# RWKV-7 chunk recurrence in 64x64 TensorE tiles, with the loop's own instructions ahead of the work placed beside it

## The chip, the cores and the metric

The program runs on one core of one Trainium2 chip. The metric is the device time of one execution in microseconds (us), as the median of the runs.

## What is computed

One encoder layer on 1024 tokens of width 1024: a projection, multi-head latent attention (8 heads) beside RWKV-7 time mixing (8 heads of 64), an output projection, cross-attention to 256 memory tokens, an MLP, and a final norm. The change touches the RWKV-7 recurrence alone:

```python
def wkv7(r, decay, k, v, a, b):
    def step(state, inp):
        rt, wt, kt, vt, at, bt = inp
        sa = jnp.einsum('bhvk,bhk->bhv', state, at)
        state = state * wt[:, :, None, :] + sa[..., None] * bt[:, :, None, :] + vt[..., None] * kt[:, :, None, :]
        return state, jnp.einsum('bhvk,bhk->bhv', state, rt)
```

The kernel doesn't step through 1024 tokens. It works in 16 chunks of 64 tokens: inside a chunk a triangular 64x64 system is solved, and from chunk to chunk the 64x64 state of each head is carried by a product with a matrix M and the addition of a matrix N.

## The kernel before, in words

All of it is written out by hand as one instruction stream for each engine. The engines meet through counted semaphores: `Steps` holds the order of named steps of one engine, `r_at(L_DVE, "st1_4")` waits for a step. Each engine works strictly in order, so a wait holds up all that stands behind it in that engine's list.

The eight heads are four *pairs* (p = 0 to 3), and a pair's two heads lie in the lower and upper 64 partitions. A pair has 8 *windows* of 128 tokens (two chunks), two windows make a *group*, so a pair has four groups g0 to g3 of four chunks each, and the loop has 16 groups. In a group TensorE (PE) does, in this order:

- `solve` (L1381): the block inverse of the two windows times their tokens; ACT copies the result (L2089).
- `local`, `other_r`, `carry` (L1392 to L1455): 56 products of 64x64 (two instructions each) that make R and Y (what the outputs read) and M and N (stacked in 128 rows, for the carry). ACT copies R and Y (L2094); DVE adds the diagonal of decays to M and N (`mt`, L2768). The diagonals (`dg`, L902) are made by POOL.
- four chunks k = 0 to 3: `state` and `outputs` (L1457, L1469) with tiles of 128x64, the old state copied by DVE into `rST` (L2778), between them the preparation of the next group: the two doubling steps of the block inverse (`double_q`, `double_z`, with masks and adds by DVE, L2741 and L2750), `scores` in k = 0 and 1 (masked by DVE, L2624), `tokens` in k = 2 and 3 (three 128x128 transposes and one product a window, copied by ACT, L1961 to L1964), and `a_v` after k = 3 (copied by ACT, L1969).

Beside this run the *slots*. Slots 0 to 43 of pair p's loop hold the preparation of pair p+1 (`prep(p + 1, s)`) and the finish of pair p-1 (`post(p - 1, s - 22)`); slots 0 to 3 of a pair are reached at the end of the group before it. For the last pair `memory_step` stands in them. Each engine calls `beside(p, s)` for each slot at its own place in its list. With t = 11 g the places are: t+4 before `local`; t+5 and t+6 before chunk 0 (DVE: t+4 and t+5 before `mt`, t+6 after it); then two slots in each chunk (`places`: t+7 + 2k and t+8 + 2k). The slots that the prediction speaks of:

- 0 to 3: PE `lw0`, `lw1`, `la0`, `la1` (L1228, one 512-column product each, into one PSUM bank, so that each waits until ACT has read the one before, L1902 and L1906); 3 DVE `kk`, `t1p`, `L`.
- 5 to 7: ACT `kksq` (L1912), PE `ks0`, `ks1` (L1231), ACT `kl0`, `kl1` (L1917). 10, 11: ACT `W`, `kf`, `Wi` (L1923, L1925, L1928), the first with a table load.
- 14 to 17: DVE `nkk`, `at`, `b`, `bt`, `kt` (L2532 to L2549). 18, 19: PE `al` (L1276) on what `bt` made, DVE masks it (L2559); then SP stores it to DRAM and reads it back in blocks.
- 26 to 30 (`SUBST`): 15 steps of two small DVE operations (L2582, L2585) and one copy (L2588): the inverse of the 16x16 blocks. SP carries it through DRAM into the tile that `double_q` of the next pair reads in g3.
- 28, 29, 32: `post` 6, 7, 10: PE L1231, ACT L1951 and L1955. 33, 34: PE `rk0`, `rk1` (L1231), DVE `bv` (L2594).
- 37 to 39: `post` 15 to 17: DVE `yn`, `yb` (L2608, L2611), PE `lg0`, `lg1` (L1228), DVE `out` (L2618).

Of the kernel before, what the change touches and what calls it, by code (L numbers as in the profile page):

```python
# [12 lines left out]
ALU = mybir.AluOpType  # L13
# [14 lines left out]
SUBST = {26: (0, 1, 2, 3), 27: (4, 5, 6, 7), 28: (8, 9, 10, 11), 29: (12, 13), 30: (14,)}  # L28
# [91 lines left out]
RP_SET = 6  # L120
# [48 lines left out]
def build(nc, x_t, mem_t, pos, wall, vecs, con_d, headw, wv_d, lora_d, out_t):  # L169
    with ExitStack() as ctx:  # L170
# [29 lines left out]
        rsm = sb("rsm", [HD, 64])  # L200
# [50 lines left out]
        rWT = [rsm[:, 32 * n:32 * n + 32].rearrange("p (c h) -> p c h", h=2) for n in range(2)]  # L251
# [10 lines left out]
        rAG, rBK, rVZ, rPG = ([wbuf(n, k).rearrange("p (h n) -> p h n", h=2) for n in range(2)] for k in range(4))  # L262
        rRY = [wbuf(n, 4).rearrange("p (c h n) -> p c h n", c=2, h=2) for n in range(2)]
# [3 lines left out]
        rDg, rMT = ssum[:, 0:512], ssum[:, 512:1024]  # L267
        rST = tmp[:, :, :].rearrange("p a (c h n) -> p (a c) h n", h=2, n=HD)
# [257 lines left out]
        P_ACT = Steps(sem("prep_act"), each(["tw0", "tw1", "ta0", "ta1", "kksq", "kl0", "kl1", "W", "kf", "Wi", "wt0", "wt1", "afirst"]))  # L526
# [7 lines left out]
        l_pe, l_act, l_dve, l_pool = ["sc0_0", "sc0_1", "tok0_0", "tok0_1", "akv0_0", "akv0_1"], [], ["sc0_0", "sc0_1"], []  # L534
        l_act += [f"{x}0_{w}" for w in range(2) for x in ("ag", "bk", "vz")] + [f"akv0_{w}" for w in range(2)]
# [4 lines left out]
        for p in range(PAIRS):  # L540
            for g in range(NW // 2):
                ab = [f"{p}_{2 * g + k}" for k in range(2)]
                more = g < NW // 2 - 1 or p < PAIRS - 1
                nx = [f"{p}_{2 * g + 2 + k}" if g < NW // 2 - 1 else f"{p + 1}_{k}" for k in range(2)]
                for x in ("pg", "ry"):
                    l_act += [f"{x}{v}" for v in ab]
                l_pe += [f"{x}{v}" for x in ("pg", "lo") for v in ab] + [f"{x}{v}" for v in ab for x in ("ry", "mn")]
                l_pool += [f"dg{v}" for v in ab]
                l_dve += [f"mt{p}_{g}"]
                for k in range(4):  # L550
                    c = 4 * g + k
                    if c < NC - 1:
                        l_dve += [f"st{p}_{c}"]
                    l_pe += ([f"y{p}_{c}", f"st{p}_{c}"] if k == 0 else
# [5 lines left out]
                    if more and k < 2:  # L560
                        l_dve += [f"sc{nx[k]}"]
                    if k == 3:
                        l_act += [f"y{p}_{g}"]
# [2633 lines left out]
```

## Time and profile before

| | us |
|---|---|
| median of 3 runs | 1725.84 (1721.74 to 1727.79) |
| the profiled execution's own time | 1721.01 |
| its span | 1718.9 |
| PE busy | 1651.7 (96%) |
| DVE busy | 1122.1 (65%) |
| ACT busy | 869.8 (51%) |
| POOL busy | 767.1 (45%) |
| the recurrence loop with what leads into it | 437 to 712.6 |

The page gives one execution: how long each engine had an instruction in work, the chain of work that ended last, and the groups of instructions that cost most. For a change inside the loop the shares over the span say little. What is read here is the timeline of single groups, where the stretch from one `solve` (L1388) to the next is the time of a group. A PE instruction's time holds about 0.2 us in which it is under way in the array, so the pitch of its instructions has to be taken from starts, or from a run of x instructions less the length of one. An fp32 product is two instructions.

### The profile page before, as it was taken

The page shows a single profiled execution, that of the slowest core. Times are in us where ns is not written, and L with a number is a line of the kernel's source. Part 1 is how long each engine was busy: PE and PEld are TensorE (multiplying, and loading weights), DVE is VectorE, ACT ScalarE, POOL GpSimd, SP SyncE. Part 2 cuts the span into 40 slices and gives each one's busy share as a digit, 9 for nine tenths or more (in the row PEclk, how much of TensorE's full clock was granted, in tenths as well). Part 3 has the DMA queues.
Part 4 walks back from the last instruction along what each step waited for, and adds up shares of the span by engine and source line. Part 5 has one row for each costly group of instructions (what it writes and reads, how often), then busy time and mean ns, then how long its engine had stood idle before and what let it go on. Part 6 is the DMA issues. An engine that isn't in the chain of part 4 may idle for free.

```text
span 1718.9 us, 30289 instructions
## 1 busy us (share of the span) xinstructions
PE 1651.7 (96%) x11840; PEld 1275.3 (74%) x11840; DVE 1122.1 (65%) x1728; ACT 869.8 (51%) x1687; POOL 767.1 (45%) x555
## 2 busy tenths in 40 slices
PE   8999999988989888999999999999999999999997
PEld 6676777655666567688977677788888888888886
DVE  8744344336466675633687769887858866784788
ACT  5323333354425444511453467766667566666763
POOL 4210212011211012313493257868768695867771
PEclk9999999998899999999999999999999999999999
DMA  6100010001121223332302003020202212120202
GB/s 242 37 25 22 25 47 1 22 6 37 27 56 28 47 40 112 136 111 73 111 25 74 1 1 98 14 86 26 74 27 72 63 37 92 31 74 25 74 1 98
DMA packets 82841, 94.45 MB, mean 55 GB/s; under 512 B 53776, under 2 KB 56336, under 8 KB 82704
## 3 DMA queue, kind: packets, MB, share of 16 engines
q1 hardware_dynamic: 82704, 92.57, 17.2%
q8 instruction: 93, 1.52, 0.4%
q14 instruction: 44, 0.36, 0.1%
HBM read 82.57 MB, written 9.98 MB: 54 GB/s over the span
## 4 chain that ended last, share of the span: by engine, by line
PE 77%; DVE 12%; ACT 4%; issue 3%; DMA 2%; POOL 2%; SPq 0%; DVEq 0%; ACTq 0%; POOLq 0%
PE PS L1727 39%; PE PS L1054 8%; PE PS L969 5%; PE PS L1155 3%; PE PS L1194 2%; PE PS L1173 2%; PE PS L1683 2%; PE PS L1228 2%; PE PS L1519 1%; PE PS L1661 1%; PE PS L1231 1%; POOL sa L917 1%; DVE H L2915 1%; PE PS L1363 1%; DVE xn L2333 1%
## 5 line engine op out<-in xcount | busy, mean ns | idle before, releaser
L1727 PE MATMUL PS<-memr,wsp 128*128 128x512 f32 x1488 | 357.6, 391 | 1.4 <-DVE memr L2897 1.4
L1727 PEld LDWEIGHTS PS<-memr,wsp 128*128 128x128 f32 x1488 | 278.7, 188 | 63.6 <-DVE memr L2897 3.6
L932 POOL TENSOR_TENSOR wsp<-sa,wsp 128x512 fp32r<-128x512 f32 x120 | 165.9, 1386 | 167.4 <-ACT wsp L2155 167.2
L1727 PE MATMUL PS<-memr,wraw_r 128*128 128x512 f32 x744 | 181.6, 393 | 0.5 <-DVE memr L2897 0.5
L1727 PEld LDWEIGHTS PS<-memr,wraw_r 128*128 128x128 f32 x744 | 140.5, 189 | 31.6 <-DVE memr L2897 1.2
L1727 PE MATMUL PS<-tmp_r,wsp 128*128 128x512 f32 x564 | 147.2, 395 | 2.5 <-DVE tmp_r L2897 2.3
L1054 PE MATMUL PS<-xn,wsp 128*128 128x512 f32 x576 | 146.3, 400 | 2.4 <-DVE proj L2378 1.5
L2897 DVE TENSOR_TENSOR memr<-PS,memr 128x512 fp32r<-128x512 f32 x185 | 126.2, 682 | 33.8 <-ACT PS L2193 33.8
L823 POOL CAST wsp<-wraw 128x1024 fp32r<-128x1024 f32 x24 | 28.2, 1175 | 239.2 <-PE PS L1054 112.5
L2915 DVE TENSOR_TENSOR H<-PS,H 128x512 f32<-128x512 f32 x160 | 108.2, 686 | 40.3 <-PE PS L1727 24.3
L1862 ACT ACTIVATE H<-PS,mst 128x128 f32<-128x128 f32 (+3 forms) x64 | 47.4, 741 | 165.1 <-DVE mst L2462 165.1
L1054 PEld LDWEIGHTS PS<-xn,wsp 128*128 128x128 f32 x576 | 104.4, 188 | 35.3 <-issue 15.7
L1727 PEld LDWEIGHTS PS<-tmp_r,wsp 128*128 128x128 f32 x564 | 105.4, 188 | 28.2 <-DVE tmp_r L2897 4.0
L2184 ACT CAST memr<-sa 128x512 fp32r<-128x512 f32 x114 | 70.3, 617 | 109.1 <-PE PS L1727 74.5
L932 POOL TENSOR_TENSOR wraw_r<-sa,wraw_r 128x512 fp32r<-128x512 f32 x64 | 88.4, 1384 | 52.8 <-ACT wraw_r L2155 52.8
L969 PE MATMUL PS<-xn,wsp 128*128 128x512 f32 x480 | 109.9, 390 | 1.1 <-issue 1.1
L917 POOL TENSOR_TENSOR sa<-sa 128x512 f32<-128x512 f32 x64 | 92.2, 1443 | 34.1 <-DMA sa<-in_weights_dram 32.2
L969 PEld LDWEIGHTS PS<-xn,wsp 128*128 128x128 f32 x480 | 90.0, 188 | 20.6 <-issue 2.0
L2193 ACT COPY PS<-sa 128x512 f32<-128x512 f32 x175 | 102.0, 583 | 3.1 <-DVE con_r L2897 1.8
L2462 DVE TENSOR_REDUCE mst<-PS 128x1 f32<-128x128 f32 (+3 forms) x64 | 48.2, 754 | 83.2 <-PE PS L1158 83.0
L2841 DVE TENSOR_TENSOR sa<-sa 128x512 f32<-128x512 f32 x80 | 93.9, 1176 | 6.6 <-ACT sa L2134 6.6
L932 POOL TENSOR_TENSOR wsp<-sbx,wsp 128x512 fp32r<-128x512 f32 x66 | 88.6, 1344 | 11.1 <-ACT wsp L2155 11.1
(384 smaller groups left out, 3438.1 us busy)
## 6 DMA issues: line engine op xcount, KB each, us to landing
sa<-in_weights_dram SPq DMA_DIRECT2D x40, 512.0 KB, 4.3
wraw<-in_weights_dram SPq DMA_DIRECT2D x24, 512.0 KB, 3.8
sa<-in_weights_dram SPq DMA_DIRECT2D x48, 256.0 KB, 2.8
H<-in_x_dram SPq DMA_DIRECT2D x16, 512.0 KB, 7.1
sbx<-in_weights_dram SPq DMA_DIRECT2D x32, 256.0 KB, 2.9
H<-in_weights_dram SPq DMA_DIRECT2D x8, 512.0 KB, 6.9
out_dram<-sbx SPq DMA_DIRECT2D x16, 256.0 KB, 2.1
a_dram<-H SPq DMA_DIRECT2D x16, 128.0 KB, 2.5
```

Source lines behind the costliest of these rows:

```text
L917: nc.gpsimd.tensor_tensor(out, a, b, op).then_inc(W_SUM.sem, W_SUM.one(name))
L932: nc.gpsimd.tensor_tensor(w[:, 1, :], w_source(g), w[:, 0, :].bitcast(F32), ALU.subtract).then_inc(mw_rest, 1)
L969: last = nc.tensor.matmul(PS[:, bank + half, :], wsp[:, k, kt, a, :], src[:, at, b, HALF * half:HALF * half + HALF], start=(i == 0 and (a, ...
L1054: last = nc.tensor.matmul(PS[:, bank, :], wsp[:, u % 2, kt, a, :], xn[:, kt, b, HALF * half:HALF * half + HALF], start=(kt == 0 and (a, b) ...
L1155: nc.tensor.matmul(PS[:, b + part, 0:n], mQ[:, win(q)], mK[:, HALF * part:HALF * part + n], start=True, stop=(part < q // 4))
L1727: last = nc.tensor.matmul(PS[:, bank_of(g), :], w[:, a, win(k)], x[:, b, :], start=(k == 0 and (a, b) == (0, 0)), stop=(k == ROWS - 1 and ...
L2184: nc.scalar.copy(x_split_of(d)[:, 0, :], x_source(d)).then_inc(mx_head, 1)
L2193: nc.scalar.copy(PS[:, PS_BANKS + d % 2, :], x_source(d)).then_inc(mx_staged, 1)
L2462: m(nc.vector.tensor_reduce(mNeg[h % 2][:, q:q + 1], two(2 * (q % 2))[:, 0:P * (q + 1)], AX_X, ALU.max, negate=True), f"m{h}_{q}")
L2841: nc.vector.tensor_tensor(out, a, b, op).then_inc(X_SUM.sem, X_SUM.one(name))
L2897: nc.vector.tensor_tensor(x[:, 1, :], source, x[:, 0, :].bitcast(F32), ALU.subtract).then_inc(mx_rest, 1)
L2915: out(nc.vector.tensor_tensor(tile, a, b, ALU.add), f"{kind}{part}_{v}")
```

## The change

- Every product of the recurrence becomes 64x64. A head's state lies in its own 64 partitions; `state` multiplies it by M alone and adds to N, which `given(p, c)` has summed into the same bank just before (4 products a chunk). The decay is no longer a diagonal in M: DVE multiplies the old state by it while it adds the bank (`scalar_tensor_tensor`). POOL's `dg` is gone, and M is copied by ACT (`mt`).
- `local`, `other_r` and `carry` become `carry(p, g)` (M and the local outputs, 24 products) and `reads(p, g)` (8 products), which go round the four tiles. R gets its r by an addition on DVE (`r`), Y by one on DVE at k = 3 (`y`) instead of ACT's copy.
- `scores`, `tokens` and `a_v` take a whole group at once, in k = 0, 1 and 2. `tokens` is 32 products with the identity or the mean filter instead of 6 transposes and 2 products. ACT copies with four instructions of 256 columns and one for `a_v`, and does it ahead of the slots of that chunk; DVE masks the scores with one instruction of 768 columns at k = 0, ahead of the slots.
- `places`: t+5 and t+6 come with t+7 and t+8 behind chunk 0. t+4 stays ahead of it, on DVE behind `r`. The substitution moves from slots 26 to 30 to slots 27 to 30.

```diff
-SUBST = {26: (0, 1, 2, 3), 27: (4, 5, 6, 7), 28: (8, 9, 10, 11), 29: (12, 13), 30: (14,)}
+SUBST = {27: (0, 1, 2, 3), 28: (4, 5, 6, 7), 29: (8, 9, 10, 11), 30: (12, 13, 14)}
...
-            return range(11 * g + 7 + 2 * k, 11 * g + 9 + 2 * k)
+            return range(11 * g + (7 + 2 * k if k else 5), 11 * g + 9 + 2 * k)
...
+            def quad(out, h, c, left, right, start, stop):
+                return nc.tensor.matmul(PS[HD * h:HD * h + HD, out[0], out[1]:out[1] + CH], left, right, start=start, stop=stop)
...
+            def carry(p, g):
+                for s in range(2):
+                    r_at(L_ACT, f"pg{p}_{2 * g + s}")
+                    for h, c in QUADS:
+                        quad((c, CH * s), h, c, rPG[s][chunk(c), h, 0:HD], rBKs[g % 2][chunk(c), s, 0, cols(h)], True, True)
+                    for h, c in QUADS:
+                        quad((c, P + CH * s), h, c, rPG[s][chunk(c), h, HD:P], rSC[s][chunk(c), h, 0, :], True, False)
+                    for h, c in QUADS:
+                        last = quad((c, P + CH * s), h, c, rVs[g % 2][chunk(c), s, h, :], rSC[s][chunk(c), h, 2, :], False, True)
+                last.then_inc(L_PE.sem, L_PE.one(f"mn{p}_{g}"))
...
+            def given(p, c):
+                n, s = c % 2, c // 2 % 2
+                if c % 4:
+                    r_at(L_PE, f"o{p}_{c - 1}")
+                elif p or c:
+                    r_at(L_DVE, f"y{p}_{c // 4 - 1}" if c else f"y{p - 1}_{NW // 2 - 1}")
+                e = c // 4 % 2
+                for k, right in enumerate((rPG[s][:, :, HD:P], rVs[e][:, s])):
+                    for h in range(2):
+                        last = quad((5 - n, 0), h, n, rBKs[e][chunk(n), s, k, cols(h)], right[chunk(n), h, :], k == 0, False)
+                last.then_inc(L_PE.sem, L_PE.one(f"n{p}_{c}"))
             def state(p, c):
...
+                if c % 4 == 0:
+                    r_at(L_ACT, f"mt{p}_{c // 4}")
+                r_at(L_PE, f"n{p}_{c}")
                 if c >= 1:
                     r_at(L_DVE, f"st{p}_{c - 1}")
...
+                    last = quad((5 - c % 2, 0), h, h, rMT[cols(h), c % 2, c // 2 % 2, :], rST[cols(h), c, :], False, True)
...
                     beside(p, t + 4)
...
+                    carry(p, g)
+                    reads(p, g)
+                    given(p, 4 * g)
                     for k in range(4):
                         c = 4 * g + k
...
                         if c < NC - 1:
                             state(p, c)
...
+                        outputs(p, c)
                         if more:
                             for n in range(2):
                                 (double_z if k % 2 else double_q)(k // 2, *following(p, g, n))
...
+                        if k < 3 and c < NC - 2:
+                            given(p, c + 1)
+                        if more and k < 3:
+                            (scores, tokens, a_v)[k](*group_after(p, g))
+                        for s in places(g, k):
+                            beside(p, s)
```

ACT's list of a group, and then DVE's:

```diff
                         nc.scalar.copy(rPG[w % 2].rearrange("p h n -> p (h n)"), PS[:, 2 + w % 2, 0:256]).then_inc(
                             L_ACT.sem, L_ACT.one(f"pg{p}_{w}"))
+                    r_at(L_PE, f"mn{p}_{g}")
+                    nc.scalar.copy(rMT.rearrange("p c s n -> p c (s n)"), PS[:, 0:2, 0:P]).then_inc(
+                        L_ACT.sem, L_ACT.one(f"mt{p}_{g}"))
...
+                    nc.scalar.copy(rY.rearrange("p c s n -> p c (s n)"), PS[:, 0:2, P:2 * P]).then_inc(
+                        L_ACT.sem, L_ACT.one(f"ly{p}_{g}"))
                     beside(p, t + 4)
...
                     for k in range(4):
...
+                        if more and k in (1, 2):
+                            (tokens, a_v)[k - 1](*group_after(p, g))
+                        for s in places(g, k):
+                            beside(p, s)
...
-                    for s in (t + 4, t + 5):
-                        beside(p, s)
-                    r_at(L_POOL, f"dg{p}_{ab[1]}")
-                    r_at(L_PE, f"mn{p}_{ab[1]}")
...
-                    beside(p, t + 6)
+                    r_at(L_PE, f"lr{p}_{g}")
+                    nc.vector.tensor_tensor(rR, PS[:, 2:4, 0:P].rearrange("p c (s n) -> p c s n", s=2),
...
+                    beside(p, t + 4)
                     for k in range(4):
                         c = 4 * g + k
                         if c < NC - 1:
                             r_at(L_PE, f"st{p}_{c}")
...
+                            nc.vector.scalar_tensor_tensor(rST[:, c + 1], rST[:, c], rWT[p % 2][:, c:c + 1],
+                                                           PS[:, 5 - k % 2, 0:CH], ALU.mult, ALU.add).then_inc(
                                 L_DVE.sem, L_DVE.one(f"st{p}_{c}"))
...
                         if more:
                             for n in range(2):
                                 (added_z if k % 2 else masked_q)(k // 2, *following(p, g, n))
...
+                        if more and k == 0:
+                            masked_scores(*group_after(p, g))
+                        for s in places(g, k):
+                            beside(p, s)
```

## Rows read from the trace of the kernel before

**Rows 1.** Engines by stretch, one group each, then the loop: busy us (instructions), granted clock, DMA.

```profile
core 0: us, PE busy (x) PEld busy (x) DVE busy (x) ACT busy (x) POOL busy (x), PEclk, DMA share, GB/s
490.00:509.70 19.70, 15.99 (x308) 12.44 (x304) 13.47 (x48) 3.71 (x13) 2.92 (x5) 0.83 0.21 33
526.20:540.90 14.70, 13.53 (x302) 10.31 (x304) 9.19 (x21) 11.35 (x23) 3.55 (x3) 1.00 0.02 4
540.90:556.10 15.20, 13.45 (x370) 11.54 (x366) 12.23 (x26) 4.86 (x15) 3.15 (x2) 1.00 0.25 44
556.10:574.70 18.60, 15.77 (x316) 11.00 (x312) 14.47 (x50) 8.71 (x18) 2.98 (x5) 1.00 0.22 34
574.70:592.90 18.20, 17.46 (x312) 11.11 (x308) 10.68 (x21) 6.33 (x18) 1.18 (x2) 1.00 0.33 83
642.20:656.20 14.00, 13.10 (x304) 9.93 (x300) 8.82 (x19) 5.51 (x15) 1.18 (x2) 1.00 0.82 245
```

**Rows 2.** Waits of the loop: who waited for whom, us in total, times, longest.

```profile
PE PS L1465 <- DVE ssum L2768: 8.5, 9, 2.5
PE PS L1350 <- ACT sc_s L1964: 7.4, 15, 1.2
```

**Rows 3.** Timeline of PE in pair 1's g1: start us, us, engine, line, shape, count.

```profile
540.92 1.19 PE L1388 MATMUL PS<-sc_s,H 64*64 64x128 f32 x16
...
543.50 0.70 PE L1445 MATMUL PS<-sc_s 64*64 64x64 f32 x26
...
550.97 0.39 PE L1465 MATMUL PS<-tmp,ssum 128*64 128x64 f32 x3
...
551.46 0.68 PE L1363 MATMUL PS<-H 64*64 64x64 f32 x16
```

**Rows 4.** Timeline of pair 1's g0 (solve at 526.21): table load, W, Wi on ACT.

```profile
534.38 1.28 ACT L1923 ACT_TABLE_LOAD   x1
...
535.68 1.06 ACT L1923 ACTIVATE sa<-sa 128x1024 f32<-128x1024 f32 x1
...
537.59 1.04 ACT L1928 ACTIVATE sa<-sa 128x1024 f32<-128x1024 f32 x1
```

**Rows 5.** Timeline of pair 1's g1 (solve at 540.92): b, bt, mt, al, the scores' mask.

```profile
541.77 1.22 DVE L2542 TENSOR_TENSOR sa<-sa 128x1024 f32<-128x1024 f32 x1
...
544.31 0.69 DVE L2768 TENSOR_TENSOR ssum<-PS,ssum 128x512 f32<-128x512 f32 x1
...
545.95 1.10 PE L1276 MATMUL PS<-sa 64*64 64x64 f32 x31
...
547.77 0.55 DVE L2624 TENSOR_TENSOR sc_w<-PS,con 128x384 f32<-128x384 f32 x1
547.91 1.15 PE L1276 MATMUL PS<-sa 64*64 64x64 f32 x32 [0.45 <-DVE H L2559]
```

**Rows 6.** Timeline of pair 1's g2 (solve at 556.13): substitution, its copy, rk0 and rk1.

```profile
558.21 0.19 DVE L2582 TENSOR_TENSOR sc_s<-sc_s 128x28 f32<-128x28 f32 x1
...
566.98 0.38 DVE L2588 COPY sc_s<-sc_s 128x256 f32<-128x256 f32 x1
...
568.77 1.12 PE L1231 MATMUL PS<-proj,con 128*128 128x512 f32 x2
...
570.68 1.12 PE L1231 MATMUL PS<-proj,con 128*128 128x512 f32 x2 [0.23 <-DVE proj L2594]
```

**Rows 7.** Timeline of pair 1's g3 (solve at 574.69): yn, lw0, tokens of one window, la1.

```profile
573.16 1.28 DVE L2608 SCALAR_TENSOR_TENSOR proj<-proj,vec,mO_odd 128x1024 f32<-128x1024 f32 x1
...
585.07 1.12 PE L1228 MATMUL PS<-proj,sc_s 64*128 64x512 f32 x2
586.12 0.33 PE L1338 MATMUL PS<-con,sa 128*128 128x128 f32 x1
...
587.03 1.12 PE L1228 MATMUL PS<-proj,sc_s 64*128 64x512 f32 x2
...
590.86 1.12 PE L1228 MATMUL PS<-proj,sc_s 64*128 64x512 f32 x2
```

More of the change, by code:

```diff
@@ L119 @@
 POST = 22
-RP_SET = 6
 SPLITS = ((10, 4), (14, 2))
@@ L1345, in a_v @@
-            def a_v(p, w):
-                s = w % 2
-                r_at(L_ACT, f"vz{p}_{w}")
-                for h in range(2):
-                    for c in range(2):
-                        last = nc.tensor.matmul(PS[chunk(c), s, HD * h:HD * h + HD], rSC[s][chunk(c), h, 1, :],
-                                                rVZ[s][chunk(c), h, HD:P], start=True, stop=True)
-                last.then_inc(L_PE.sem, L_PE.one(f"akv{p}_{w}"))
+                if p or g:
+                    r_at(L_ACT, f"ly{p}_{g - 1}" if g else f"ly{p - 1}_{NW // 2 - 1}")
@@ L1354, in double_q, with a_v @@
+            def a_v(p, g):
+                r_at(L_ACT, f"bk{p}_{g}")
+                for h in range(2):
+                    for s in range(2):
+                        for c in range(2):
+                            last = nc.tensor.matmul(PS[chunk(c), s, HD * h:HD * h + HD], rSC[s][chunk(c), h, 1, :],
+                                                    rVs[g % 2][chunk(c), s, h, :], start=True, stop=True)
+                last.then_inc(L_PE.sem, L_PE.one(f"akv{p}_{g}"))
             def double_q(lv, p, w):
@@ new lines, in reads @@
+            def reads(p, g):
+                for s in range(2):
+                    for h, c in QUADS:
+                        last = quad((2 + c, CH * s), h, c, rPG[s][chunk(c), h, 0:HD], rSC[s][chunk(c), h, 0, :], True, True)
+                last.then_inc(L_PE.sem, L_PE.one(f"lr{p}_{g}"))
+            def given(p, c):
[9 more added lines that the diff above has]
+                last.then_inc(L_PE.sem, L_PE.one(f"n{p}_{c}"))
@@ L1576, in attention_end @@
                     pair_factors(PAIRS - 1, s - 6)
-            for stage in (scores, tokens, a_v):
-                for w in range(2):
-                    if stage is scores and w or stage is tokens and not w:
-                        keep_busy(2 + w, 2 * P)
-                    stage(0, w)
-            pe.wait_ge(rp_dve, RP_SET)
+            scores(0, 0)
+            for bank in (2, 3):
+                keep_busy(bank, 2 * P)
+            tokens(0, 0)
+            keep_busy(4, HALF)
+            a_v(0, 0)
+            pe.wait_ge(rp_dve, 2)
             for bank in (2, 4, 3):
@@ L2075, in _ @@
                     values(h // 2 + 1)
-            for w in range(2):
-                tokens(0, w)
-            for w in range(2):
-                a_v(0, w)
+            tokens(0, 0)
+            a_v(0, 0)
             for s in range(4):
```

372 lines of the change are left out of this document (132 added, 240 removed).

## The prediction

> **What bounds the kernel now.** I read the page's busy shares first (PE 96% of the span), but this change touches only the loop from 437 to 712.6 us, so the view that counts is the timeline cut at each `solve`: sixteen groups of 10.6 to 19.7 us. Pair 1's four take 14.7, 15.2, 18.6 and 18.2 us [rows 1]. In them PE has an instruction in work for 13.5 to 17.5 us and DVE for 9 to 14.5, so PE has little room, but neither engine is full. The list of waits says what PE stands still for: `state` waits for `mt` on DVE (8.5 us in all), `a_v` for ACT's copies of the tokens (7.4 us) [rows 2]. The rest of a group is a chain that runs from engine to engine: bt, then al (PE), a mask (DVE), al again [rows 5]; the substitution of thirty small DVE operations [rows 6]; four projections into one bank, each 1.93 us after the last (585.07 to 590.86, three links), with the tokens of a window, 0.91 us, hidden between two of them [rows 7]. The reader should see there that much of PE's work in the loop today fills time that a chain would take anyway.
>
> **PE's own work gets shorter.** Prices, from [rows 3]: an instruction that goes round the four tiles has a pitch of (0.70 - 0.22)/25 = 0.019 us, one that alternates between two tiles 0.031, `solve` takes 0.92 in all, and `state` with `outputs` (eight in 128x64) 0.49. Per group:
> - local products and carry: 112 instructions become 64 at 0.0205 (1.3 us for 2.3): -1.0.
> - `state` and `outputs`, now two tiles: 4 x (0.49 - 0.25) = -1.0; `given` adds 4 x 8 x 0.031 = +1.0.
> - `tokens`: 2 x 0.91 = 1.8 [rows 7] becomes 64 x 0.0205 = 1.3: -0.5. No row shows this product with the identity; it is the same form as the carry's.
> - `scores`, 1.0, becomes 16 x 0.0205 + 16 x 0.0275 (a 128-column instruction, between the carry's price and solve's 0.057) = 0.8: -0.2.
> - the waits of [rows 2], (8.5 + 7.4)/16 = -1.0 if nothing replaces them. `state` in chunk 0 waits for its own `given` to leave the array: +0.25.
> Together about -2.5 us a group of PE time. DVE is even: `mt` 0.69, four copies of 0.28 and two masks of 0.55 [rows 5] go, and `r` 0.45, `y` 0.45, four of 0.2 and a mask of 768 columns (0.95, by twice the 384 columns less one fixed part) come. ACT is 0.4 less. POOL loses 1.2 us a group in which it waits anyway: 0. DVE's copies and memsets ahead of the loop lay in its idle time: 0.
>
> Whether two passes with the identity could be one is settled by the Trainium skill, "TensorEngine Tiling (Array Packing)", section Restrictions and Gotchas: column tiling excludes transpose mode for fp32. The same page's rule that changing the tiling mode drains TensorE speaks for the change. The trace agrees in so far as eight 128x64 instructions amid 64x64 ones take 0.061 each. Its section PSUM Bottleneck, that tiling speeds TensorE but not the evacuation, speaks against; what follows is that case in this kernel's own numbers.
>
> **What the new order puts behind what.** I place each engine's list against the others for pair 1, from `solve` = 0. Common front: solve 0.9, carry from 1.1 to 2.15 with ACT's two copies of 0.37 between, reads and `given` to 2.7, state c0 at 3.0, `r` on DVE at 2.7 to 3.15, outputs, q, `given`, `scores` to 4.9 (5.1 where the slots of the group before hold ACT a little). DVE cannot touch slot t+4 before 3.15, since it stands behind `r`; today it does t+4 and t+5 while PE solves.
> - **g0.** ks0 follows at 5.1, and ks1 one link later; PE leaves chunk 0 at 8.0. State, z, given and tokens end at 10.8. ACT's four token copies now stand ahead of slot 10: 10.95 to 12.15. Only then come the table load (1.28), W and kf (1.91 for the two) [rows 4]: 15.35. Behind them stands `a_v`'s copy, 0.37, for which the next solve waits: 15.8. Today the load starts 8.2 after solve (534.38 - 526.21). Against 14.7: **+1.1**.
> - **g1.** Today b and bt run at 541.77 to 544.3, while PE is in `local` and `carry`, so al starts 5.0 after solve [rows 5]. After: r 3.4, `at` 4.6, state, two masks and the scores' mask 6.3, then b and bt (1.25 each) 8.8. PE has nothing but al from 5.1 on and waits 3.7 us. First al 8.85 to 9.95, mask, second 10.85 to 11.95; today it leaves at 8.1. What is left is shorter, 5.75 for 7.1: 17.7. Against 15.2: **+2.5**. SP's stores to DRAM start 4 us later, and the blocks are back 2.7 us into g2, before DVE wants them: 0.
> - **g2.** The substitution takes 7.5 us of DVE (558.21 to 567.36, less 1.7 of other work between, and one of the fifteen steps before it) [rows 6]. It stands whole between chunk 0 and chunk 1's state: 6.0 to 13.6. PE has vs0, vs1, z and tokens, to 10.8, then waits 3 us. State c2, q and a_v to 15.7; rk0 and rk1 one link apart [rows 6] and no tokens left to hide in it: 18.7; state, z and DVE's adds: 20.1. Against 18.6: **+1.5**. The inverse is in DRAM later too; today its loads begin 4.7 us behind the copy and land about 9.5 behind it, so after at 3.0 of g3, just ahead of q at 3.3: 0, at most 0.5.
> - **g3.** yn and yb (1.28 each [rows 7]) today start before solve; after they stand behind `r`: 3.15 to 5.75, masks to 7.45, out0 8.15, so lg1 8.2 to 9.25. State, z, tokens 12.05, q and a_v 13.95, then lw0 to la1, 6.95 with nothing hidden in it: 20.9. Against 18.2: **+2.7**.
>
> **The sum.** Pair 1: 1.1 + 2.5 + 1.5 + 2.7 = +7.8. Pair 0 has attention's factors between ks0 and ks1, and no `post` work: 0 + 2.5 + 1.5 + 0.2 = +4.2. Pair 2's g3 has no projections (today 14.0 [rows 1]); the same placement gives 14.9: 1.1 + 2.5 + 1.5 + 0.9 = +6.0. Pair 3 has no preparation. In g0 to g2 the gain on PE is eaten by memory casts that stand behind `a_v`'s copy on ACT: 0. In g3 yn, yb and one cast come ahead of the last states: +3.4. What leads into the loop has fewer products: -0.8. Total +20.6 us. Against the execution's own time, 1721.0 + 20.6 = 1741.6; the median lies 4.8 above that execution, so **1746 us**.
>
> The bounds. The placement ignores contention and costs every handover at 0.05 to 0.2 us; 1 us a group either way is what I can't exclude, over the twelve groups with a placed chain 12 us: 1733 to 1758.
>
> **Rivals.**
> 1. *The clock falls in the new holes.* In pair 0's g2 the granted clock was 0.83, so part of it ran at 1.2 GHz instead of 2.4, and it took 19.7 for pair 1's 18.6 [rows 1]; PE had stood still there for 2.5 us before `state` [rows 2]. The change makes holes of 3 to 3.7 us in three g1 and three g2. At 1.1 to 2 us each, +7 to +12: about 1755. Against it: such a hole need not bring a fall, as g3 with 1.2 us holes shows 1.00. The Trainium skill, "TensorE: Matmul & The Clock Gate", section HAM oscillation, warns of just such gaps; no row here shows how long a gap it takes.
> 2. *PE's own work decides.* If the chains have more slack than I place, because ACT and DVE reach their slots before PE does, a group gets the -2.5 us in whole where no chain stands and about half elsewhere: 16 x 1.5 = -24, so 1702. It decides if b and bt end before 5.1 after solve in g1, that is, if `r` is not late. For it: PE is the fullest engine in every row of [rows 1]. Against it: the order of DVE's list is plain in the code, and `r` needs the carry.
> 3. *Both cancel.* The shorter work fills the chains as before, the holes are half of what I place: +0 to +9, so 1726 to 1733. It is also what comes out if the four-tile pitch falls below 0.0205.
> 4. *The new products don't overlap.* At 0.031 for all: 128 instructions x 0.01 = +1.3 a group more, 1760. Against it, the carry's pitch.
>
> **How the numbers follow.** My forecast (1733 to 1758) 0.50; rival 1 0.15; rival 2 0.18; rival 3 0.12; rival 4 0.05. The range 1714 to 1762 leaves out most of rival 2 and the ends of 1 and 4, together 0.2. A measurement of this kernel tells 0.3%, 5.2 us, from no change. Faster than 1720.7: rival 2 and the foot of rival 3, 0.19. Within: 0.10. Slower than 1731: 0.71.
>
> **What would show it.** Right: in g1 DVE's b starts after the scores' mask, and the first al starts 8 to 9 us after solve; in g0 the table load of W starts behind four copies, about 12 after solve; in g2 chunk 1's state is added only after the inverse's copy; in g3 nothing of the loop lies between lw0 and lw1; groups of 15.8, 17.7, 20.1 and 20.9. POOL and DMA are not late for anyone. Wrong: groups g0 to g2 no longer than today; tokens over 1.6 us; a group of pair 3's g1 that is longer than 14, for which I have no mechanism; a clock under 0.9 in a g1.

## The result, and the profile after

| | before | after |
|---|---|---|
| median, same chip, 4 runs each, us | 1723.79 (1720.16 to 1727.79) | 1760.86 (1754.55 to 1766.56) |
| the profiled execution's own time | 1721.01 | 1754.55 |
| its span | 1718.9 | 1752.7 |
| the loop, first `solve` to its end | 456.9 to 712.6 | 459.6 to 747.1 |

The ratio is 1.0214, 95% interval 1.0168 to 1.0259: slower by 2.1%, 37 us in the medians and 33.8 in the two spans. The loop's end is 34.55 later, so the work behind the loop gives back 0.75. In what follows a *hole* is a stretch in which PE stands still, and the *slow level* is the granted clock of 1.2 GHz, against 2.4 GHz at full clock.

The first section of the page of after: busy time of each engine over the span.

```profile
span 1752.7 us, 31349 instructions
PE 1640.3 (94%) x12418; PEld 1273.4 (73%) x12418; DVE 1119.1 (64%) x1724; ACT 857.6 (49%) x1619; POOL 746.4 (43%) x523
```

PE works 11.4 us less than before and the span is 33.8 longer. The same cut into groups as [rows 1]: pair 0's g1, then pair 1's g0 to g3.

```profile
core 0: us, PE busy (x) PEld busy (x) DVE busy (x) ACT busy (x) POOL busy (x), PEclk, DMA share, GB/s
477.60:499.40 21.80, 16.40 (x400) 15.17 (x400) 14.06 (x24) 3.94 (x12) 3.69 (x3) 0.61 0.12 27
538.10:553.00 14.90, 11.37 (x343) 8.98 (x342) 9.23 (x20) 10.26 (x18) 1.22 (x1) 1.00 0.02 3
553.00:574.50 21.50, 16.20 (x402) 14.89 (x403) 14.09 (x25) 4.47 (x13) 3.75 (x3) 0.68 0.14 28
574.50:595.30 20.80, 15.25 (x344) 11.09 (x345) 13.04 (x52) 8.36 (x15) 1.22 (x1) 0.92 0.25 39
595.30:617.10 21.80, 17.59 (x336) 10.52 (x336) 12.34 (x23) 5.03 (x12) 0.00 (x0) 0.88 0.25 65
```

Two things are to be seen. In pair 1's g0, at full clock in both kernels, PE is busy 11.37 us for 13.53 [rows 1], and the group is as long as before. In g1 the granted clock, 1.00 before, is 0.61 and 0.68, so most of the group ran at the slow level.

All sixteen groups, `solve` to `solve` (the last to the loop's end), in us, and my forecast of the difference:

| | g0 | g1 | g2 | g3 |
|---|---|---|---|---|
| pair 0 before, after | 17.81, 18.05 | 15.22, 21.81 | 19.78, 20.82 | 16.46, 17.81 |
| difference (forecast) | +0.2 (0) | +6.6 (+2.5) | +1.0 (+1.5) | +1.4 (+0.2) |
| pair 1 before, after | 14.71, 14.88 | 15.21, 21.51 | 18.56, 20.86 | 18.22, 21.78 |
| difference (forecast) | +0.2 (+1.1) | +6.3 (+2.5) | +2.3 (+1.5) | +3.6 (+2.7) |
| pair 2 before, after | 14.71, 16.70 | 15.22, 19.16 | 19.32, 20.86 | 14.06, 13.93 |
| difference (forecast) | +2.0 (+1.1) | +3.9 (+2.5) | +1.5 (+1.5) | -0.1 (+0.9) |
| pair 3 before, after | 18.45, 17.20 | 12.82, 13.81 | 14.54, 15.10 | 10.53, 13.24 |
| difference (forecast) | -1.3 (0) | +1.0 (0) | +0.6 (0) | +2.7 (+3.4) |

With the lead-in (+2.65, forecast -0.8) this makes the 34.55. The waits of the loop, to be set beside [rows 2] (us in total, times, longest):

```profile
PE PS L1390 <- DVE tmp L2718: 16.4, 6, 6.0
PE PS L1263 <- issue: 10.6, 3, 3.5
PE PS L1384 <- ACT sc_s L1925: 7.8, 4, 2.2
...
PE PS L1344 <- ACT sc_s L1920: 2.6, 5, 0.6
```

The wait for `mt` on DVE (8.5 us) is gone, and that for the tokens' copies is smaller (7.4 before). In their place stand 16.4 us for a state (L2718), 12.9 of them in the three g2 where DVE adds it behind the substitution, three times 3.5 ahead of `al` (L1263), and 7.8 for the copy of `a_v` (L1925) ahead of `solve`. The view names nobody for `al`; the timeline does.

Timeline of pair 1's g1 (`solve` at 552.96), the rows that answer to [rows 5]: POOL's `rt`, DVE's `nkk`, `solve` on PE, PE's carry, `r` and the scores' mask on DVE, b, bt, al, its mask, al again.

```profile
551.78 2.36 POOL L853 TENSOR_TENSOR sa<-proj,sa 128x1024 f32<-128x1024 f32 x1 [51.03 <-ACT sa L1882]
...
552.68 2.54 DVE L2479 SCALAR_TENSOR_TENSOR sa<-sa 128x1024 f32<-128x1024 f32 x1 [1.24 <-ACT sa L1884]
...
552.96 1.20 PE L1384 MATMUL PS<-sc_s,H 64*64 64x128 f32 x16 [2.19 <-ACT sc_s L1925]
...
555.21 1.08 PE L1390 MATMUL PS<-sc_w,sc_s 64*64 64x64 f32 x32
...
556.35 0.42 DVE L2705 TENSOR_TENSOR sc_s<-PS,sa 128x256 f32<-128x256 f32 x1 [1.13 <-PE PS L1390]
...
560.13 0.96 DVE L2570 TENSOR_TENSOR sc_w<-PS,con 128x768 f32<-128x768 f32 x1 [1.45 <-PE PS L1314]
561.01 1.22 DVE L2489 TENSOR_TENSOR sa<-sa 128x1024 f32<-128x1024 f32 x1
562.26 1.22 DVE L2493 TENSOR_TENSOR sa<-sa 128x1024 f32<-128x1024 f32 x1
...
563.58 1.62 PE L1263 MATMUL PS<-sa 64*64 64x64 f32 x32 [3.52 <-issue]
...
565.24 0.76 DVE L2506 TENSOR_TENSOR H<-PS,con 128x256 f32<-128x256 f32 x2 [0.62 <-PE PS L1263]
566.05 1.65 PE L1263 MATMUL PS<-sa 64*64 64x64 f32 x26 [0.85 <-DVE H L2506]
```

`al` starts 0.10 behind the end of bt: that is the wait without a name. Ahead of `solve` PE had stood still for 2.19 us; the carry's 32 instructions then take 1.08 where the same row in g2, at full clock, has 0.65 (shown further down), and `al` takes 1.62 for 1.15 [rows 5].

Pair 2's g1 (`solve` at 633.81) shows the same lists without the slow level behind `solve`. The carry, the scores' mask and al:

```profile
635.66 0.65 PE L1390 MATMUL PS<-sc_w,sc_s 64*64 64x64 f32 x32
...
638.63 0.96 DVE L2570 TENSOR_TENSOR sc_w<-PS,con 128x768 f32<-128x768 f32 x1
...
642.08 1.61 PE L1263 MATMUL PS<-sa 64*64 64x64 f32 x32 [3.52 <-issue]
```

The hole ahead of `solve` is 2.19 us here too, but the carry runs at full clock, DVE does not wait for PE's scores (1.45 us in pair 1), and `al` starts 8.3 us after `solve` and not 10.6, behind the same hole of 3.52 us. So 2.3 us of the two longer g1 come from the slow level ahead of `al`: a slow PE makes DVE's chain longer too.

### The profile page after: what moved, and what is told of

Its sections match the earlier page's. It is cut to its first block, busy times and chain, and to the rows that moved or that the text cites. A ratio compares the mean times of both kernels' runs of the same rounds, so it can differ in the third digit from the quotient of the medians.

```text
span 1752.7 us, 31349 instructions
## 1 busy us (share of the span) xinstructions
PE 1640.3 (94%) x12418; PEld 1273.4 (73%) x12418; DVE 1119.1 (64%) x1724; ACT 857.6 (49%) x1619; POOL 746.4 (43%) x523
## 4 chain that ended last, share of the span: by engine, by line
PE 76%; DVE 13%; ACT 5%; issue 4%; DMA 1%; SPq 0%; DVEq 0%; ACTq 0%
PE PS L1686 38%; PE PS L1041 8%; PE PS L956 5%; PE PS L1142 3%; PE PS L1390 3%; PE PS L1181 2%; PE PS L1160 2%; PE PS L1215 2%; PE PS L1642 2%; PE PS L1487 1%; PE PS L1620 1%; DVE sa L2787 1%; PE PS L1218 1%; DVE H L2861 1%; PE PS L1263 1%
```

## The experiments

Each kernel was timed beside the kernel before on the same chip. The sessions were on different chips and their medians of before go from 1718.9 to 1723.8 us, so it is the ratios to before that can be set beside each other. A trace is of one execution: in the 14 traces pair 0's copy behind the substitution, ahead of the loop, stands anywhere from 426.0 to 433.6 us, so the traces are read group by group. Two theories stood at first: *order* (the places of slots, tokens and substitution cost the time, the products are worth 1 us or more a group) and *product* (the new products or their chains cost it).

### The two halves of the change, each alone

`tiles_old_order` has the new products with the slots where the kernel before has them:

```diff
-SUBST = {27: (0, 1, 2, 3), 28: (4, 5, 6, 7), 29: (8, 9, 10, 11), 30: (12, 13, 14)}
+SUBST = {26: (0, 1, 2, 3), 27: (4, 5, 6, 7), 28: (8, 9, 10, 11), 29: (12, 13), 30: (14,)}
...
-            return range(11 * g + (7 + 2 * k if k else 5), 11 * g + 9 + 2 * k)
+            return range(11 * g + 7 + 2 * k, 11 * g + 9 + 2 * k)
...
 # PE: t+5 behind carry, t+6 behind given; ACT: t+4 to t+6 ahead of chunk 0; DVE: t+4, t+5 ahead of r, t+6 behind
```

> The changed kernel with its 64x64 products, but with every slot back where the kernel before has it: DVE's t+4 and t+5 ahead of r, t+6 behind it, PE's and ACT's t+5 and t+6 ahead of chunk 0, two slots a chunk from t+7, and the substitution in slots 26 to 30. If the order costs the time (my theory), this is at or under the kernel before: PE's shorter own work gives up to 1 us a group, so 1705 to 1724 us. If the 64x64 products themselves cost it (rival), it stays at 1745 to 1760.

`before_new_order` is the kernel before with the new slot places alone; its scores, their masks, the tokens and `a_v` stay where they were:

```diff
-                    for s in (t + 4, t + 5):
-                        beside(p, s)
                     r_at(L_POOL, f"dg{p}_{ab[1]}")
...
-                    beside(p, t + 6)
+                    beside(p, t + 4)
...
 # and t+5, t+6 behind chunk 0 on PE, ACT and DVE; SUBST as in the change
```

> The kernel before with its old products, but in the new order of slots: DVE's t+4 behind mt, t+5 and t+6 behind chunk 0 on all engines, the substitution in slots 27 to 30. Order theory: most of the 37 us, so 1745 to 1765, with the first al (L1276's place) 8 us or more after solve in g1. Product theory: within 0.3% of before, 1719 to 1729.

Measured: `before_new_order` 1772.97 (1767.97 to 1777.17), ratio 1.0300 [1.0254, 1.0345]; `tiles_old_order` 1745.07 (1739.9 to 1747.5), ratio 1.0129 [1.0080, 1.0177]. The new slot places do harm by themselves, and more of it (3.0%, above the 1745 to 1765 us of my theory) than the whole change (2.1%). The 0.9% between them is not the products' alone, since the whole change also moves scores, tokens and `a_v`. Its g1 are 21.8, 20.8 and 21.1 us, at 0.76 and 0.84 in the rows here, and each has a hole of 3.1 us ahead of `al`, 8.3 after `solve` (645.41 in pair 2), so the hole and its clock need none of the new products:

```profile
481.02:502.80 21.78, 17.60 (x369) 15.16 (x367) 12.46 (x26) 3.84 (x14) 3.35 (x2) 0.76 0.21 38
...
557.64:578.45 20.81, 16.46 (x368) 14.04 (x366) 12.39 (x26) 4.79 (x15) 3.19 (x2) 0.84 0.22 40
```

```profile
645.41 1.84 PE L1276 MATMUL PS<-sa 64*64 64x64 f32 x32 [3.09 <-issue]
```

But `tiles_old_order` fell into the product theory's range. Either the products cost something, or an order was left in it that the kernel before has not. Some of it was left: tokens and `a_v` still stood in a block in chunks 1 and 2, ACT's copies ahead of its slots, and on DVE the scores' mask ahead of both slots of chunk 0. The later runs take this up.

### Single steps of the order, undone one at a time

> The changed kernel, but DVE does slot t+4 (and in g0 and g1 slot t+5) ahead of r, while PE solves. Order theory: b and bt end about 4 us after solve instead of 9.5, the hole on PE in g1 goes, and the clock with it: g1 from 21.5 to 15 to 16, three of them, and g3 2 us less: 1735 to 1743. If DVE's order is not the cause: 1755 to 1765.

```diff
+                    beside(p, t + 4)
+                    if g < 2:
+                        beside(p, t + 5)
                     r_at(L_PE, f"lr{p}_{g}")
...
-                    beside(p, t + 4)
...
-                            beside(p, s)
+                            if g >= 2 or s != t + 5:
+                                beside(p, s)
```

> The changed kernel with ACT doing the slots of chunks 1 and 2 ahead of the copies for tokens and a_v. In g0 the table load, W and kf then need not wait for PE's tokens: I expect the load at 9 instead of 11.3 us after solve, nkk 2 us earlier, the hole of 2.2 us ahead of g1's solve gone and g1's clock higher. If this late ACT chain is what makes g1 long (the run with DVE's slots first left it at 19.5 to 21): g0 and g1 together 3 to 5 us shorter in three pairs, 1745 to 1752. If it is only DVE's order: 1757 to 1764.

```diff
-                        if more and k in (1, 2):
-                            (tokens, a_v)[k - 1](*group_after(p, g))
                         for s in places(g, k):
                             beside(p, s)
+                        if more and k in (1, 2):
+                            (tokens, a_v)[k - 1](*group_after(p, g))
```

`dve_and_act_first` has both edits.

> The changed kernel with both: DVE's t+4 (and t+5 in g0 and g1) ahead of r, and ACT's slots ahead of its copies in chunks 1 and 2. If both stand in one chain (W and kf on ACT, nkk, b and bt on DVE, al on PE), the two together give more than their sum (0 for DVE alone): g1 at 15 to 17 us, 1732 to 1742. If they are independent: the same as ACT's change alone.

`subst_undone` has the line `SUBST` of the kernel before. `tokens_spread_alone` moves the tokens and `a_v` (PE's part is shown, ACT's copies move with it):

```diff
-                        if more and k < 3:
-                            (scores, tokens, a_v)[k](*group_after(p, g))
-                        for s in places(g, k):
+                        if more and k == 0:
+                            scores(*group_after(p, g))
+                        first, *others = places(g, k)
+                        beside(p, first)
+                        if more and k >= 2:
+                            (tokens, a_v)[k - 2](*group_after(p, g))
+                        for s in others:
                             beside(p, s)
```

> The changed kernel with the substitution's 15 steps back in slots 26 to 30, everything else as changed. The same table also places them beside the attention heads for pair 0, where in the changed kernel's trace TensorE stood still for 4.7 us behind a row maximum that had been put off, and the first scores started 13.0 us after the substitution's copy instead of 10.9. If the move of the substitution costs there: the lead-in gets 2 to 3 us shorter (first solve about 31 us after that copy instead of 33.6), groups g2 change by less than 1 us each since the four steps of slot 26 only move from behind chunk 0 to behind r, and the median is 1757 to 1759. If the move is nothing, the lead-in stays at 33.6 and the median within 1 us of the changed kernel's 1760.9. If the substitution is what makes the changed kernel slow at all (a theory I hold unlikely), 1735 or less.

> The changed kernel with all slots where the change puts them (three behind chunk 0, t+4 behind r), but the tokens in k = 2 and a_v in k = 3, each between that chunk's two slots, on TensorE and on ACT. It takes out one part of the new order alone: that tokens and a_v are done early and in a block. With the old slot places that spreading was worth 20 us (1742.2 to 1721.8). If the packing costs by itself, g0's table load comes about 1.2 us earlier, g3 has the tokens between lw1 and la0 again and g3 of pairs 0 and 1 is 2 to 4 us shorter, and the median is 1741 to 1751. If the hole of g1 (b and bt behind the scores' mask) and of g2 carries the loss and the packing costs only where the slots stand in the old places, the median is 1754 or more and g1 stays at 19 to 22 us.

| | us | ratio to before |
|---|---|---|
| after | 1760.86 | 1.0214 [1.0168, 1.0259] |
| dve_slots_first | 1761.39 (1757.14 to 1768.07) | 1.0237 [1.0187, 1.0287] |
| act_slots_first | 1756.27 (1754.09 to 1769.92) | 1.0200 [1.0183, 1.0218] |
| dve_and_act_first | 1755.08 (1751.76 to 1756.97) | 1.0192 [1.0171, 1.0213] |
| subst_undone | 1757.12 (1751.15 to 1759.07) | 1.0213 [1.0177, 1.0250] |
| tokens_spread_alone | 1758.94 (1751.07 to 1760.03) | 1.0205 [1.0165, 1.0245] |

No step of the five, undone, moves the ratio by more than its interval. The figure for the case that the step matters was missed in four of them: `dve_slots_first` (1735 to 1743), `dve_and_act_first` (1732 to 1742), `act_slots_first` (1745 to 1752, and 1756.3 lies between its two ranges) and `tokens_spread_alone` (1741 to 1751). Only `subst_undone` came where it was put, 1757 to 1759. The likely reason is that I took a step's price as if the others stayed as they were. In `dve_slots_first` b stands ahead of `r`, but in g1 `nkk` comes late and slow, and `r` with it. `nkk` waits for ACT's kf, which has fallen behind the token copies, and runs beside POOL's `rt`:

```profile
555.39 2.36 POOL L853 TENSOR_TENSOR sa<-proj,sa 128x1024 f32<-128x1024 f32 x1 [54.07 <-ACT sa L1882]
...
556.30 2.54 DVE L2479 SCALAR_TENSOR_TENSOR sa<-sa 128x1024 f32<-128x1024 f32 x1 [1.24 <-ACT sa L1884]
```

`subst_undone` shows one thing in the trace alone, the lead-in. The table `SUBST` also places pair 0's steps beside the attention heads. In after PE waits there 4.69 us for a copy (L1830) that stands behind a row maximum, and restarts at the slow level; with the old table it waits 2.64. Two rows each of PE's timeline, the restart and the first scores, after and then subst_undone:

```profile
429.32 1.55 PE L1181 MATMUL PS<-H,tmp 128*64 128x128 f32 x12 [4.69 <-ACT H L1830]
...
438.86 0.34 PE L1310 MATMUL PS<-sa 64*64 64x64 f32 x8
```

```profile
429.48 0.88 PE L1181 MATMUL PS<-H,tmp 128*64 128x128 f32 x12 [2.64 <-ACT H L1830]
...
436.88 0.34 PE L1310 MATMUL PS<-sa 64*64 64x64 f32 x8
```

The first `solve` is at 456.04, 3.55 earlier than after and 0.9 earlier than before (456.94); this is the -0.8 of my sum. The other traces bear it out. From the substitution's copy to the first scores it is 12.4 to 13.2 us in the seven kernels with the new table, `before_new_order` among them, and 10.8 in the others (11.0 in before, 12.1 in one). In the medians it cannot be told from nothing.

### Does the clock carry the surplus of g1?

`hole_kept_busy` is after with products that nobody reads, three (512 columns) behind the scores in g1 and two at the end of g0, in pairs 0 to 2.

```diff
                             (scores, tokens, a_v)[k](*group_after(p, g))
+                        if p < PAIRS - 1 and g == 1 and k == 0:
+                            for _ in range(3):
+                                keep_busy(6, HALF)
```

> The changed kernel with three products of 512 columns (3.2 us) for nothing in PE's hole of g1, between the scores and slot 18, and two (2.1 us) at the end of g0 behind chunk 3, in the pairs 0 to 2. They add 16 us of PE work, in places where PE stands still for 3.5 and 2.2 us. If the clock's fall in g1 costs time (0.61 to 0.82 granted there), this is faster than the changed kernel: 1 to 4 us for each g1, 1748 to 1756, with the clock of g1 over 0.9. If the fall costs nothing beyond the hole: 1760 to 1765.

Measured 1756.01 (1752.64 to 1764.64), ratio 1.0203 [1.0149, 1.0257]. Its windows, g1 and g2 of pair 0, then g1 of pair 1:

```profile
482.35:498.89 16.54, 13.88 (x407) 11.21 (x407) 13.71 (x24) 3.90 (x12) 3.38 (x3) 1.00 0.16 34
498.89:521.63 22.74, 15.43 (x341) 11.47 (x341) 13.04 (x51) 2.96 (x9) 1.62 (x1) 0.70 0.31 51
...
558.06:576.23 18.17, 15.51 (x407) 12.84 (x407) 14.11 (x24) 4.44 (x13) 4.03 (x3) 0.91 0.15 32
```

With 2.8 us of work added in the hole (3.2 was expected), g1 is shorter: 16.5, 18.2 and 18.1 us for 21.8, 21.5 and 19.2, at a clock of 1.00 and 0.91 in pairs 0 and 1 for 0.61 and 0.68. `al` starts 8.3 to 8.4 us after `solve` in all three, for 10.6, 10.6 and 8.3: DVE's and ACT's lists are the same, what differs is the added work and TensorE's clock. The two later g1 are near the 17.7 that I had forecast, and pair 0's is 1.2 under it. So the slow level that comes with the two holes costs a g1 1 to 5 us beyond the placed chain. The median came at the upper edge of its range (1748 to 1756), and the intervals of the two ratios overlap: over the whole program next to nothing comes back. Pair 1's g0, with work added at its end, takes 16.4 for 14.9, g2 of pairs 0 and 2 takes 22.7 and 23.3 for 20.8 and 20.9, g3 of these pairs 20.1 and 17.2 for 17.8 and 13.9, with clocks of 0.70 to 0.84 in these four. A hole that is filled leaves the next one.

### The rest of the order, with the old slot places

`tiles_old_order_act` adds the edit of `act_slots_first` to `tiles_old_order`. `tiles_spread` is `tiles_old_order` and puts scores, tokens and `a_v` between the two slots of chunks 0, 2 and 3, on PE and ACT, instead of ahead of the slots of chunks 0, 1 and 2. PE's part:

```diff
+                        first, *others = places(g, k)
+                        beside(p, first)
+                        if more and k != 1:
+                            {0: scores, 2: tokens, 3: a_v}[k](*group_after(p, g))
+                        for s in others:
+                            beside(p, s)
```

> The run tiles_old_order (1745 us: all slots where they were before the change) with ACT's slots ahead of its copies as well. That run left one part of the new order in: a group's tokens and a_v in chunks 1 and 2, with ACT's copies ahead of the slots. If that part is what still holds it 22 us above the kernel before, this comes to 1720 to 1732. If the 64x64 products cost the rest: 1740 to 1748.

> The 64x64 products, all slots at the places of the kernel before, and the group's tokens in chunk 2 between its two slots, a_v in chunk 3 between its two slots, the scores in chunk 0 behind the first slot: work of the loop lies between the projections of g3 again, and ACT's W comes ahead of the copies. Order theory: PE's shorter own work can now show, 0.5 to 1 us a group: 1706 to 1720. Product theory: 1735 or more.

Measured: `tiles_old_order_act` 1742.21 (1734.05 to 1743.43), ratio 1.0111 [1.0080, 1.0143]; `tiles_spread` 1721.8 (1718.63 to 1728.37), ratio 1.0017 [1.0001, 1.0032]. The kernel with all the new products is within 0.2% of the kernel before once the order is the old one but for the scores' mask on DVE: the product theory, which asked for 1735 or more, has fallen. The order theory's own ranges were missed too, by 10 us (1720 to 1732 for `tiles_old_order_act`, which fell where the products were to blame) and by 2 (1706 to 1720). Windows of `tiles_spread`, pair 1's g0 to g2:

```profile
527.06:541.37 14.31, 11.52 (x341) 9.14 (x341) 10.25 (x21) 11.22 (x19) 2.38 (x1) 1.00 0.01 3
541.37:556.38 15.01, 11.21 (x400) 10.07 (x400) 11.83 (x26) 3.93 (x11) 3.00 (x2) 1.00 0.18 38
556.38:580.46 24.08, 16.72 (x345) 11.98 (x345) 12.34 (x49) 7.97 (x14) 0.82 (x1) 0.86 0.20 24
```

PE is busy 2.0 and 2.2 us less than before in g0 and g1 at full clock, and the groups are 0.4 and 0.2 us shorter; the g1 of pairs 0 and 2 are longer than before, 16.8 and 16.4 for 15.2, at 0.90. Two waits remained: 1.73 to 1.75 us in each g1 for the mask of the first al, and 5.68 in this g2 for `r`, which stood behind eight substitution steps, the first of which waited for the read from DRAM:

```profile
561.75 0.18 DVE L2536 TENSOR_TENSOR sc_s<-sc_s 128x15 f32<-128x15 f32 x1 [6.11 <-DMA sc_s<-a_dram]
...
565.99 0.48 PE L1390 MATMUL PS<-sc_s,tmp 64*64 64x64 f32 x4 [5.68 <-DVE sc_s L2714]
```

`spread_between` moves the scores' mask on DVE behind the first slot of chunk 0, where the kernel before has it, and g1's tokens to chunk 1. `r_first_in_g2` also puts `r` ahead of the substitution in g2:

```diff
+                    late = g == 2 and p < PAIRS - 1
+                    if not late:
                         for s in (t + 4, t + 5):
                             beside(p, s)
                     r_at(L_PE, f"lr{p}_{g}")
...
+                        first, *others = ((range(t + 4, t + 6), range(t + 6, t + 11))[k] if late and k < 2
+                                          else places(g, k))
```

> The kernel with the new products, the old slot places and tokens and a_v spread (1721.8 us beside 1719.3 for the kernel before), with two more edits of order: on DVE the scores' mask goes behind the first slot of chunk 0 and not ahead of both, since in all three g1 TensorE waited 1.73 to 1.75 us for the mask of the first al; and in g1 the tokens go into chunk 1, since a_v waited 0.62 us there for ACT's copies. If what is left is order, g1 gets 1.2 to 1.8 us shorter in three pairs and the median falls by 4 to 6, to 1716 to 1718, just below the kernel before. If g1 is limited elsewhere (r behind b and bt, or the scores' later use), the median stays at 1720 to 1723.

> The kernel with the new products, the old slot places, spread tokens and the scores' mask between the slots (1714.8 us beside 1718.9 for the kernel before), with one edit on DVE in g2 of pairs 0 to 2: r comes first, the first eight substitution steps behind chunk 0's masks, the other seven behind chunk 1's. In that kernel's trace TensorE stood still 3.7, 2.6 and 5.6 us in the three g2 for r, which stood behind substitution steps that themselves waited for the blocks' read from DRAM (2.1 to 5.1 us), and the granted clock of those groups was 0.74 to 0.91. If r behind a DMA wait is what is left, those holes go to under 1 us, since TensorE has chunk 0's outputs, q, scores and a projection to do meanwhile; the three groups fall from 19.6, 19.4 and 23.1 to 16 to 18 us, the clock there is 0.9 or more, and the median is 1704 to 1708. If the substitution's own length decides (it then holds up chunk 1's or 2's state, as in the changed kernel, where it held chunk 1's), the hole only moves, g2 stays at 19 or more, and the median is 1712 to 1716.

Measured: `spread_between` 1714.81 (1706.54 to 1721.26), ratio 0.9968 [0.9948, 0.9988]; `r_first_in_g2` 1713.43 (1706.47 to 1721.77), ratio 0.9950 [0.9933, 0.9968]. Both are faster than either kernel of the case. In the first g1 is 14.2, 13.8 and 13.2 us (before 15.2), and the median is 1 us under its range (1716 to 1718). Here `al` starts 4.4 after `solve`, and PE's shorter work shows in the group's time. In the second the three g2 are 18.3, 19.1 and 18.6 for 19.6, 19.4 and 23.1, but the hole only moved, as the rival had it (1712 to 1716; my own figure was 1704 to 1708). PE's waits of the loop, in `spread_between` and then in `r_first_in_g2`:

```profile
PE PS L1391 <- DVE sc_s L2715: 14.0, 6, 5.6
```

```profile
PE PS L1391 <- DVE tmp L2731: 7.8, 4, 3.0
...
PE PS L1360 <- DMA H<-xt_dram: 5.8, 3, 3.4
PE PS L1391 <- DVE sc_s L2717: 2.0, 3, 0.7
```

14.0 us for `r` become 2.0, and in their place come a state behind the substitution (7.8 for 2.6) and g3's first q, which waits for the inverse that is now later in DRAM (5.8 for 2.2).

## Why the prediction was right, and where its sum was not

The forecast was 1746, slower; measured were 1761, slower. That is 1.1 us inside the upper end of the range (1714 to 1762) and above the forecast's own 1733 to 1758: the way and the mechanism were right, and that the number came inside owes something to luck, since the rise was 37 us for 20. Point by point:

- **The placement**: what I had placed behind what stands there in all four groups; the lengths fit less well. g1 stands above: b and bt follow the scores' mask and al follows them. In pair 2 al starts 8.3 us after `solve`, for 8.9; in pairs 0 and 1, at the slow level, it starts at 10.6, outside the 8 to 9 that I had named as a sign. g0: the table load of W stands behind the four token copies, 11.3 after `solve` (538.08) for 12.2:

```profile
548.13 0.37 ACT L1917 COPY sc_s<-PS 128x256 f32<-128x256 f32 x1 [1.93 <-PE PS L1390]
548.40 0.38 ACT L1918 COPY sc_s<-PS 128x256 f32<-128x256 f32 x1
548.67 0.67 ACT L1920 COPY ssum<-PS 128x256 f32<-128x256 f32 x2
549.35 1.28 ACT L1882 ACT_TABLE_LOAD   x1
```

  g2 (the carry's row first, then the inverse's copy): chunk 1's state is added right behind the copy, and PE goes on 13.5 after `solve` (574.47); I had 13.6. The hole is 3.5 us in pairs 1 and 2, and 6.0 in pair 0:

```profile
576.19 0.65 PE L1390 MATMUL PS<-sc_w,sc_s 64*64 64x64 f32 x32
...
587.27 0.38 DVE L2535 COPY sc_s<-sc_s 128x256 f32<-128x256 f32 x1
587.57 0.28 DVE L2718 SCALAR_TENSOR_TENSOR tmp<-tmp,rsm,PS 128x64 f32<-128x64 f32 x1
...
587.99 0.48 PE L1390 MATMUL PS<-tmp,ssum 64*64 64x64 f32 x4 [3.47 <-DVE tmp L2718]
```

  g3: nothing of the loop stands between lw0 and lw1; lw0 at 13.0 after `solve` (595.33) for 13.95. From lw0 to `solve` it took 8.8 for 6.95, since the last two ran at the slow level, 2.07 for 1.12:

```profile
608.35 1.12 PE L1215 MATMUL PS<-proj,sc_s 64*128 64x512 f32 x2
610.31 1.12 PE L1215 MATMUL PS<-proj,sc_s 64*128 64x512 f32 x2 [0.84 <-ACT sa L1861]
...
612.27 2.07 PE L1215 MATMUL PS<-proj,sc_s 64*128 64x512 f32 x2
615.11 2.07 PE L1215 MATMUL PS<-proj,sc_s 64*128 64x512 f32 x2 [0.78 <-ACT sa L1865]
```

- **The mis-sized term is g1**: +16.8 us for the three, forecast +7.5. I had "Pair 1: 1.1 + 2.5 + 1.5 + 2.7", which takes the placed chain at full clock; the clock stood apart as rival 1, at 1.1 to 2 us a hole and a chance of 0.15. They were not alternatives. The placement makes the hole and the hole goes with the slow level: 0.61, 0.68 and 0.82 in the three g1. `hole_kept_busy` has g1 at 16.5 at full clock and 18.2 and 18.1 near it, so the placed chain of 17.7 was about right; what the three g1 took beyond it, at the slow level, is 4.1, 3.8 and 1.5 us, where I had 2 at most. The sign that I had named for being wrong, "a clock under 0.9 in a g1", is there. The Trainium skill, "TensorE: Matmul & The Clock Gate", section HAM oscillation, tells of idle gaps of TensorE behind which the next work starts at the slow level. The trace agrees for the hole of 3.52 us, behind which `al` takes 1.6 to 2.0 for 1.15 in all three g1.
- **The lead-in**: +2.65 for -0.8. The step "What leads into the loop has fewer products" looked only at products; that `SUBST` is also read beside the attention heads was missed. `subst_undone` has the -0.9. The -0.8 itself holds: from the first scores to the first `solve` it takes 19.15 us there for 19.9 in before.
- **PE's own work**: -2.5 us a group was forecast and -2.0 to -2.2 of busy time came, at full clock. The pitch was not right in detail. The carry's 32 instructions are 0.65 in all, so (0.65 - 0.22)/31 = 0.014 for the 0.0205 that I took; no row gives that 0.0205, and my own working from [rows 3] had 0.019. A group's 64 token instructions take 1.2 us at full clock for the 1.3 reckoned, and 1.6 to 1.7 in the three g1, which meets the sign "tokens over 1.6" there, by the clock and not by the pitch. That such work would be eaten was right: in g0 of pair 1 2.2 us less of PE gave nothing.
- **g0 of pair 1**: +0.2 for +1.1. Tokens and chunk 1 were shorter by that pitch, so the copies came at 10.05 for 10.95. g0 of pair 2 cost 2.0, at 0.85.
- **g2, g3 and pair 3**: +4.9, +4.8 and +3.0 for +4.5, +3.8 and +3.4.

So the surplus over the profiled time of 1741.6 (1754.55, 13 us) is g1 9.3, the lead-in 3.5, and 0.2 of all else: the other groups 1.2, less 1.0 behind the loop.

Rival 2, PE's own work decides (0.18), is refuted for the change: its condition, b and bt before 5.1 after `solve`, never came. Where it does come, in `tiles_spread`, `spread_between` and `r_first_in_g2`, bt ends 3.3 to 3.7 after `solve`. The first is no faster than before; in the other two g1 is 1.0 to 2.6 us shorter and the time 0.3 to 0.5% below before, not the 24 us I gave it. Rival 3 had a second condition, a pitch below 0.0205. It came and its time (1726 to 1733) did not, and the holes were not halved: 3.5 us for the 3.7 placed in g1. Rival 4 is refuted by the pitch; its price was also summed wrongly, as 1.3 us a group gives 1762 over twelve groups and 1767 over sixteen, not 1760. The lower bound 1733 and rival 3's 1733 are 1 to 2 us too low by my own terms (1734, and 1735 by +9).

What stays open: how much of the order's loss belongs to which slot. From `dve_and_act_first` to `tiles_old_order_act` go 13 us, in which the slots t+5 and t+6 of all three engines and the substitution move together. With the old places, the spreading of scores, tokens and `a_v` is worth 20 us (1742.2 to 1721.8). With the new ones the spreading of tokens and `a_v` moves nothing that can be told from the noise. I have not separated these. Nor was the order of `r_first_in_g2` tried with the old products, so its last gain can't be divided between products and order. The likely reason, that any one hole left brings the slow level back to its neighbours, is only argued; `hole_kept_busy` fits it in g1 and g2.

## What to carry to other kernels

Shortening an engine's own work brings nothing where a chain through other engines sets the length. Here the new places of the slots alone cost 3%, and the new products gained their 0.3 to 0.5% only when nearly all of the old order was back. When you place a list against another and find that TensorE will stand still as long as here (2.2 to 3.5 us), don't price the hole and the clock as two cases: take the work behind the hole at the slow level too (behind the 2.2 us hole it came in two of three g1, behind the 3.5 us hole in all three), and let it lengthen the other engines' chains that wait for that work. Look up every reader of a table of places before pricing an edit to it, and don't price the undoing of one step by its share in the sum: with several holes in a row, closing one moved nothing that could be measured.

## What the runs showed of the hardware that I had not expected

- A DVE operation on two SBUF tiles of 1024 columns (`nkk`) takes 2.54 us where it starts while POOL multiplies 1024 columns (2.36), in both fences above that show it, and about 1.21 in all four cases of before; in pair 1 it starts there 0.21 after POOL's has ended. The POOL operation is as long with it as without (2.36 and 2.37).
- fp32 products of 64x64 that go round the four tiles have a pitch of 0.014 us an instruction, not the 0.0205 of my sum.
- The same hole of 2.19 us before `solve` in g1 is followed by the slow level in pairs 0 and 1 and by full clock in pair 2 (the carry's 32 instructions 1.08 and 0.65 us in pairs 1 and 2). Why is open.
